# First RMS norm over partitions instead of rows: inputs loaded with features on partitions, sums by a product with ones

## The reference, cut to what matters

```python
def rms_norm(x, g):
    y = x * rsqrt(mean(x * x, axis=-1) + RMS_EPS)
    return y * g

u = rms_norm(x, g_pre) @ w_in + b_in          # q, k, v, pool input, two gates
# windowed attention over k, v (new tokens also see cache_k_win, cache_v_win)
# causal pooling over the pool input (new tokens also see state_pool)
m = sigmoid(ga) * (attn @ w_attn_up) + sigmoid(gp) * (pool @ w_pool_up)
h = x + rms_norm(m @ w_out, g_post_mix)
f = square(relu(rms_norm(h, g_pre_mlp) @ w_mlp_up)) @ w_mlp_down
y = h + rms_norm(f, g_post_mlp)
```

## Time and profile before

| what | value |
|---|---|
| median of 3 runs | 1433.7 us (1433.47 to 1434.33) |
| profiled execution, span from first to last instruction | 1431.3 us |
| around the span (median less span) | 2.4 us |
| PE busy | 1396.4 us, 98% |
| DVE, ACT, POOL busy | 38%, 32%, 11% |
| share of PE in the chain that ended last | 91% |

### The profile page before, as it was taken

How to read it: one execution, slowest core, us unless ns; L and a number is a source line. 1 busy time by engine, 2 the same in 40 slices (tenths; PEclk the granted TensorE clock), 3 DMA queues, 4 the chain that set the end, 5 groups by cost and what they waited for, 6 DMA issues and landing times.

```text
span 1431.3 us, 21460 instructions
## 1 busy us (share of the span) xinstructions
PE 1396.4 (98%) x8647; PEld 1366.2 (95%) x8647; DVE 543.1 (38%) x971; ACT 455.1 (32%) x891; POOL 161.8 (11%) x192
## 2 busy tenths in 40 slices
PE   6999999999999999999999999999999999999996
PEld 5999989999999999989999999999999999999986
DVE  5355541322222244687323323323223233232367
ACT  6354542311111143454224032141240321412423
POOL 3000565000000002441000000000000000000054
PEclk9999998999999999999999999999999999999997
DMA  9100000111111124130111111111011010111103
GB/s 303 39 30 16 31 16 30 49 45 44 45 45 45 45 60 118 45 96 15 32 43 50 42 42 52 36 44 59 29 59 44 29 59 29 44 58 34 56 1 125
DMA packets 28788, 74.56 MB, mean 52 GB/s; under 512 B 2722, under 2 KB 12088, under 8 KB 28703
## 3 DMA queue, kind: packets, MB, share of 16 engines
q1 hardware_dynamic: 19207, 65.84, 14.2%
q10 hardware_dynamic: 8400, 4.46, 1.2%
q0 software_dynamic: 1120, 3.39, 0.7%
HBM read 68.85 MB, written 5.92 MB: 52 GB/s over the span
## 4 chain that ended last, share of the span: by engine, by line
PE 91%; DVE 4%; DMA 2%; ACT 1%; issue 1%; POOL 0%; SPq 0%; ACTq 0%; DVEq 0%; POOLq 0%
PE ps L1238 28%; PE ps L1239 28%; PE ps L1240 28%; PE ps L1257 3%; PE ps L1388 2%; DVE acc L1201 1%; DVE hh L1206 1%; DMA xrow<-in_x_prompt 1%; DMA xre<-in_x_prompt 1%; PE ps L1451 0%; DMA xre_s<-in_x_sample 0%; DVE rsy L1090 0%; PE ps L1350 0%; DVE acc L1143 0%; PE ps L1397 0%
## 5 line engine op out<-in xcount | busy, mean ns | idle before, releaser
L1238 PE MATMUL ps<-xn,wr 128*128 128x384 f32 (+1 forms) x1344 | 443.8, 330 | 2.3 <-issue 1.5
L1239 PE MATMUL ps<-xn,wr 128*128 128x384 f32 (+1 forms) x1344 | 441.2, 328 | 0.0
L1240 PE MATMUL ps<-xn,wr 128*128 128x384 f32 (+1 forms) x1344 | 440.8, 328 | 0.0
L1238 PEld LDWEIGHTS ps<-xn,wr 128*128 128x128 f32 x1344 | 254.1, 189 | 3.7 <-issue 3.2
L1239 PEld LDWEIGHTS ps<-xn,wr 128*128 128x128 f32 x1344 | 254.1, 189 | 0.0
L1240 PEld LDWEIGHTS ps<-xn,wr 128*128 128x128 f32 x1344 | 253.8, 189 | 0.0
L1238 PE MATMUL ps<-ff,wr 128*128 128x384 f32 (+2 forms) x720 | 237.8, 330 | 0.0
L1239 PE MATMUL ps<-ff,wr 128*128 128x384 f32 (+2 forms) x720 | 236.8, 329 | 0.0
L1240 PE MATMUL ps<-ff,wr 128*128 128x384 f32 (+2 forms) x720 | 236.4, 328 | 0.0
L1126 DVE TENSOR_TENSOR ff<-sqa,ff 128x384 fp32r<-128x384 f32 (+1 forms) x96 | 51.5, 537 | 267.3 <-ACT ff L795 267.0
L1143 DVE TENSOR_TENSOR acc<-acc,ps 128x384 f32<-128x384 f32 (+2 forms) x168 | 88.6, 530 | 167.4 <-PE ps L1240 166.7
(11 more groups left out here) (215 smaller groups left out, 1619.6 us busy)
## 6 DMA issues: line engine op xcount, KB each, us to landing
raw<-in_weights SPq DMA_DIRECT2D x106, 512.0 KB, 3.5
xrow<-in_x_prompt SPq DMA_DIRECT2D x8, 512.0 KB, 9.9
xre<-in_x_prompt ACTq DMA_DIRECT2D x8, 512.0 KB, 5.7
out_y_prompt<-yrow SPq DMA_DIRECT2D x8, 512.0 KB, 2.6
bias_rev<-bias_by_distance POOLq DMA_DIRECT2D x1, 1024.0 KB, 10.4
gbc<-in_norm_pre_mix SPq DMA_DIRECT2D x1, 512.0 KB, 6.1
vcache<-in_cache_v_win POOLq DMA_DIRECT2D x1, 512.0 KB, 8.8
kcache<-in_cache_k_win SPq DMA_DIRECT2D x1, 512.0 KB, 11.1
```

Of the source, the lines that this page charges most:

```text
L1238: pe.matmul(out, wh, rh, start=(i == 0), stop=False)
L1239: pe.matmul(out, wh, rl, start=False, stop=False)
L1240: mm = pe.matmul(out, wl, rh, start=False, stop=(i == last))
```

## The change

x, the key cache and the pool state are laid out on the host with features on partitions, behind the weights (units `U_XT`, `U_XS`, `U_KC`), and the vectors as 128 columns. x is loaded as `xin [128, 8, 1088]`: for chunk 0 in four loads of two features each, for chunks 1 and 2 in one load each. The norm then sums over partitions and tiles: ACT squares feature by feature (`x_square`), DVE (chunk 0) or POOL (chunks 1 and 2) adds the eight squares to `xsum`, PE multiplies by ones (`x_total`), ACT takes the root of 128x384 (`x_root`), DVE inverts 128x384 (`x_invert`) and scales feature by feature in pairs into `xsc` (`x_scale`); ACT copies hi and DVE subtracts for lo. K groups wait per feature. All turns of x, vectors, key cache and state are gone. The residual adds x from `xre` in SBUF, loaded with features on partitions, one load a chunk (two for the last).

```diff
-            x_load(0)
-            sp.dma_start(gbc[:, :], I["norm_pre_mix"].to_broadcast([P, D])).then_inc(gbc_in, 16)
-            sp.dma_start(vecrow[:, :], I["vectors"]).then_inc(vec_in, 16)
-            x_load(1)
+            for i in range(2):
+                x_load(i, 2 * i, 2 * i + 2, 0)
+            sp.dma_start(vec[:, 0:V_EPS], I["vectors"]).then_inc(vec_in, 16)
+            unit(U_K, 0)
+            for i in range(2, 4):
+                x_load(i, 2 * i, 2 * i + 2, 0)
...
             unit(U_V, 1)
+            x_load(4, 0, KD, 1)
+            x_load(5, 0, KD, 2)
...
+            def add_x_squares(c):
+                for k in range(1, KD):
+                    pool.wait_ge(x_sq, KD * c + k + 1)
+                    pool.wait_ge(x_add, 7 * c + k - 1)
+                    w = CH[c][1]
+                    pool.tensor_tensor(xsum[:, 0:w], xsum[:, 0:w], xsq[k % 2][:, 0:w], ALU.add).then_inc(x_add, 1)
...
+            def x_square(c, k):
...
+                if k >= 3:
+                    act.wait_ge(x_add, 7 * c + k - 2)
+                act.activation((xsq[k % 2] if k else xsum)[:, 0:CH[c][1]], xin[:, k, cs(c)], ACT.Square).then_inc(x_sq, 1)
+
+            def x_root(c):
+                w = CH[c][1]
+                act.wait_ge(x_sum, c + 1)
...
+            for k in range(KD):
+                x_square(0, k)
             split(U_K)
...
+            x_root(0)
+            act.wait_ge(vec_in, 16)
+            for k in range(KD):
+                x_high(0, k)
+                if k == 1:
+                    split(U_V)
+                if k >= 3:
+                    x_square(1, k - 3)
+            for k in range(5, KD):
+                x_square(1, k)
             in_group(U_K, 0)
...
+            def x_scale(c, k0):
+                w = CH[c][1]
+                for k in (k0, k0 + 1):
+                    if KD * c + k >= 2:
+                        dve.wait_ge(x_lo, KD * c + k - 1)
+                    dve.scalar_tensor_tensor(out=xsc[k % 2][:, 0:w], in0=xin[:, k, cs(c)], scalar=vec[:, V_G0 + k:V_G0 + k + 1],
+                                             in1=xrs[c % 2][:, 0:w], op0=ALU.mult, op1=ALU.mult).then_inc(x_t, 1)
+                for k in (k0, k0 + 1):
+                    dve.wait_ge(x_hi, KD * c + k + 1)
+                    dve.tensor_tensor(xn[:, 1, k, cs(c)], xsc[k % 2][:, 0:w], xn[:, 0, k, cs(c)].bitcast(f32),
+                                      ALU.subtract).then_inc(x_lo, 1)
...
-                        dve.wait_ge(xr_t, KD * c + k + 1)
-                        dve.tensor_tensor(h, h, ps[:, 5 + k % 2, 0:w], ALU.add).then_inc(n_h, 1)
+                        if k == 0:
+                            dve.wait_ge(xr_in[c], 16 if c < NC_ - 1 else 32)
+                        dve.tensor_tensor(h, h, xre[:, k, cs(c)], ALU.add).then_inc(n_h, 1)
...
-                        x_again(st - 1, m)
```

More of the change, by code:

```diff
@@ L266, in build @@
         n_sum, n_sd, n_rs, n_t, n_h, n_sq, n_add = (sem("n_" + n) for n in ("sum", "sd", "rs", "t", "h", "sq", "add"))
-        n2_t, n2_hi, n2_lo, xr_in, xr_t = (sem(n) for n in ("n2_t", "n2_hi", "n2_lo", "xr_in", "xr_t"))
+        n2_t, n2_hi, n2_lo = (sem(n) for n in ("n2_t", "n2_hi", "n2_lo"))
+        xr_in = [sem(f"xr_in{c}") for c in range(NC_)]
         f_sq, f_hi, f_lo = sem("f_sq"), sem("f_hi"), sem("f_lo")
@@ L417, in _ @@
-            sp.dma_start(state_in[:, :], I["state_pool"][0].rearrange("b s n -> (b s) n")).then_inc(st_in, 16)
-            for r in range(5, RT):
-                x_load(r)
+            unit(U_V, 1)
+            x_load(4, 0, KD, 1)
+            x_load(5, 0, KD, 2)
+            sp.dma_start(xin[:, :, SEQ:ROWS], I["weights"][U_XS][:, 0:KD * SROWS].rearrange("p (k n) -> p k n", n=SROWS))\
+                .then_inc(x_in[5], 16)
+            sp.dma_start(kxT[:, :, 0:WIN], I["weights"][U_KC].rearrange("p (b n) -> p b n", n=WIN)).then_inc(kc_in, 16)
@@ L621, in _ @@
             act.wait_ge(eps_set, 1)
-            act.activation(rs[:, 0:1], eps, ACT.Sqrt).then_inc(x_sd, 1)
+            act.activation(xrs[0][:, 0:1], eps, ACT.Sqrt).then_inc(x_sd, 1)
             act.wait_ge(x_sd, 1)
-            x_stats(0)
-            x_stats(1)
-            x_high(0)
-            x_stats(2)
+            for k in range(KD):
+                x_square(0, k)
             split(U_K)
-            x_high(1)
-            x_stats(3)
-            x_high(2)
-            split(U_V)
-            x_stats(4)
-            x_stats(5)
-            act.wait_ge(kc_t, 1)
-            act.activation(kxT[:, :, 0:WIN], ps[:, 6:8, :].rearrange("p a (b n) -> p (a b) n", n=P), ACT.Copy)\
-                .then_inc(kc_r, 1)
-            x_high(3)
-            x_stats(6)
-            x_high(4)
-            act.wait_ge(vec_r, 1)
-            in_group(U_K, 0)
-            x_high(5)
-            x_stats(7)
-            in_group(U_V, 0)
-            x_high(6)
-            x_stats(8)
-            x_high(7)
-            in_group(U_K, 1)
-            x_high(8)
-            in_group(U_V, 1)
+            x_root(0)
[8 more added lines that the diff above has]
+                x_square(1, k)
+            in_group(U_K, 0)
+            x_root(1)
+            for k in range(KD):
+                x_high(1, k)
+                if k == 1:
+                    in_group(U_V, 0)
+                if k >= 2:
+                    x_square(2, k - 2)
+            for k in range(6, KD):
+                x_square(2, k)
+            in_group(U_K, 1)
+            x_root(2)
+            for k in range(KD):
+                x_high(2, k)
+                if k == 1:
+                    in_group(U_V, 1)
             in_group(U_K, 2)
@@ L940, in in_group @@
                                          op0=ALU.add, op1=ALU.subtract).then_inc(freed["D"], 1)
-            dve.wait_ge(gbc_in, 16)
-            x_scale(0)
-            x_scale(1)
-            x_low(0)
-            dve.wait_ge(vec_t, 1)
-            dve.tensor_copy(vec[:, 0:62], ps[:, 6, 0:62]).then_inc(vec_r, 1)
-            x_scale(2)
-            lo(U_K)
+            for k in range(1, KD):
+                dve.wait_ge(x_sq, k + 1)
+                dve.wait_ge(x_add, k - 1)
+                dve.tensor_tensor(xsum[:, :], xsum[:, :], xsq[k % 2][:, :], ALU.add).then_inc(x_add, 1)
+            lo(U_K)
+            dve.wait_ge(vec_in, 16)
+            x_invert(0)
+            x_scale(0, 0)
+            lo(U_V)
+            for k0 in (2, 4, 6):
+                x_scale(0, k0)
             dve.wait_ge(brow_p, 1)
@@ L1269, in _, with x_total, kv_group @@
-            pe.wait_ge(ident_set, 1)
-            x_turn(0)
-            pe.wait_ge(vec_in, 16)
-            turn(ps[:, 6, 0:62], vecrow[:, :], 62).then_inc(vec_t, 1)
-            x_turn(1)
+            def x_total(c):
+                pe.wait_ge(x_add, 7 * (c + 1))
+                pe.matmul(ps[:, 2 + c, 0:CH[c][1]], ones[:, :], xsum[:, 0:CH[c][1]], start=True, stop=True).then_inc(x_sum, 1)
+            def kv_group(n, c):
+                g = g_in(n, c)
+                need(n)
+                bank_free(g)
+                for k in range(KD):
+                    if n == U_K:
+                        pe.wait_ge(x_lo, KD * c + k + 1)
+                    wh, wl = wtile(n, k)
+                    rh, rl = rows(xn, k, c)
+                    out = ps[:, bank_of(g), 0:CH[c][1]]
+                    pe.matmul(out, wh, rh, start=(k == 0), stop=False)
+                    pe.matmul(out, wh, rl, start=False, stop=False)
+                    mm = pe.matmul(out, wl, rh, start=False, stop=(k == KD - 1))
+                mm.then_inc(done, 1)
@@ L1289, in _ @@
[L1289 to L1297 removed]
+            x_total(0)
+            kv_group(U_K, 0)
             kv_group(U_V, 0)
[L1299 to L1300 removed]
+            x_total(1)
             kv_group(U_K, 1)
[L1302 removed]
```

193 lines of the change are left out of this document (64 added, 129 removed).

## The result

| kernel | median, us | ratio to the kernel before (95%) |
|---|---|---|
| before, 4 runs | 1433.6 (1432.7 to 1434.3) | |
| changed, 4 runs | 1454.2 (1451.7 to 1457.7) | 1.0156 (1.0134 to 1.0178) |

The change makes the kernel 1.56% slower. The sign was forecast; the size was not: 1442.3 us was forecast, and 1454.2 lies 5.7 us above the range.

The account below looks back on a forecast made before the run. PE, busy 98% of the 1431.3 us span, was taken as the bound. 1431.3 + 16.9 (head) - 8.3 (residual stage) = 1439.9, with 2.4 around the span 1442.3 us; range 1436.5 to 1448.5.

Parts of the forecast that it names:

- The sign: Whole kernel: the change makes it slower, given 0.88.
- The five idle microseconds at the start of K1: Head: PE idle for about 5 us behind the second product with ones, at 36 to 42 us.
- the pace of the pairs: Head: K0 goes at the pace of feature pairs, 2.25 us a pair without collisions or squares, not of PE.
- The forecast's lower bound of the head: Head: if no collision and no square costs anything, the loss falls from 16.9 to 11.3 us.
- The head's size: Head: Q0 ends at 73.9 us instead of 56.99, 16.9 us later.
- Last features: 12.4: Head, load: chunk 0's last features of x land at 12.4 us, 0.4 of it for 1.5 KB runs.
- rival (b): PE at its slower level in V0 and V2/Q0: plus 3.5 to 7 us, 1446 to 1449; 13%.
- the adds' collisions: Head: scalings that meet POOL's adds take 1.36 us instead of 0.6.
- The residual stage: Residual stage: turns and waits removed from PE give a gain of 8.3 us, bounds 6 and 10.5.
- the old 4.65 us: Residual stage, chunk 1: a DVE step is 4.65 us, busy throughout, longer than a group of 320 columns (3.5).
- rival (a): Residual stage: full exclusion of DVE and POOL, chunk 1's step 6.5 us, gain 2.8, time 1447.8; 15%.
- its first sum is not late: Residual stage, chunk 0: the first sum isn't late, so the chunk gives its full 2.6 us.

Follow-up runs that it names:

- e13: Changed kernel with chunk 0's x loaded first, x's squares summed by PE, and chunk 0's sums issued ahead of the bias table's product: 1441.1 us, ratio 1.0062.
- e3: Changed kernel with chunk 0's x loaded ahead of the vectors and K's weight unit: 1449.9 us, ratio 1.0128.
- e10: Changed kernel with GpSimd's four small early loads issued behind its adds of chunk 1's squares: 1448.2 us, ratio 1.0115.
- e7: Changed kernel with unneeded products placed where PE waits in the head: 1451.9 us, ratio 1.0139.
- e4: Kernel before with only the new residual stage, POOL's adds of squares there done over one column: 1419.0 us (1 run).
- e11: Changed kernel with chunk 0's x loaded first and GpSimd's four small loads issued late: 1446.5 us, ratio 1.0104.
- e6: Changed kernel with POOL's adds of squares in head and residual stage done over one column (the narrow adds): 1432.7 us (1 run).
- e14: Changed kernel, chunk 0's x loaded first, squares of x and h summed by PE, chunk 0's sums ahead of the bias table's product: 1434.3 us, ratio 1.0018.

## Why the prediction was right or wrong

**The sign and the mechanism of the head: right, and shown.** The five idle microseconds at the start of K1 are there (5.15), so is the pace of the pairs. The forecast's lower bound of the head, without collisions, was 11.3 us, and e13, without adds, measures 11.9; that the two are so near is luck. The bound had K0 start at 20.3 and each sum behind V0; e13 starts K0 at 17.87 and takes the sums of the next chunk along with K and V, and still needs 51.0 us from there to vT's turn, where the bound had 48.0.

**The head's size: 16.9 forecast, 23.9 measured; 7.0 short.** Step by step along PE's rows:
- The product with ones: forecast at 14.0 (last add done 13.95), measured 16.96, so 3.0. The failed step is "Last features: 12.4"; ACT could square them only from 15.13. The rate was taken from the two queues of the page, as if 1.5 KB runs alone filled the queue. The vectors and the last loads of x shared the engines with GpSimd's loads. e3 and e10 show that x was late and that order alone cures it (3.9 and 4.0 us).
- The first feature of K0: 20.3 and 23.89, so 0.6 more, mostly the product with ones at the slower level (1.65 us).
- The product of chunk 1: begins at 35.9 in the forecast (36.5 is its end) and at 41.85, 2.35 more. Of these 0.65 are K0's, and 1.7 V0's, forecast at 4.2 us; it takes 5.9 (35.96 to 41.85), with its first products 0.32 us apart. This is rival (b), half true: the prediction bounded it at 3.5 us in V0 and left it out of the sum. e7 could not settle what it costs there, since it left V0 partly slow.
- The first feature of K1 0.3 more, the sum of chunk 2 0.2, the end 0.6.

The forecast gave 1.9 + 2.5 + 1.2 = 5.6 us to the adds' collisions, to squares between the hi copies and to POOL's last adds. The narrow adds show 7.1. e3 against e13, with the same loads, shows 8.2, but e13 also drops DVE's adds and starts the next sums earlier. So the term was right in kind and 1.5 us low.

**The residual stage: 8.3 forecast, 4.7 measured.** The three chunks: 1.2, -0.7 and 4.2 us, forecast 2.6, 0.5 and 5.2, so 1.4, 1.2 and 1.0 short. In chunk 1 the step that failed is the one taken at the old 4.65 us. It is 6.85, near the 6.5 of rival (a), and the sum waits 6.58 us instead of 5. The prediction had noted that the new add "reads two SBUF tiles and can lengthen POOL's adds" and charged 0.5 us for it. It also let chunk 0 keep its 2.6, because "its first sum is not late"; but its second sum was, and PE waited 1.24 us for POOL's. And it took the products behind the wait at full speed: from the second sum of chunk 1 to the next sum are 13.3 us, before 11.9. These 1.4 us are PE at its slower level behind a wait of 6.58 us, which is rival (b)'s mechanism at a place where the prediction didn't look for it. The rule of the Trainium skill ("SBUF — State Buffer", "Who interferes with whom") is that a DVE instruction with two SBUF inputs and a GpSimd one that reads SBUF exclude each other; the rival built on it had 15%. In this trace it holds: the add of x goes from 1.02 to 2.52 us a pair once it reads SBUF, and didn't move while it read PSUM. The row that I held against it, the lo part of 1.21 us that didn't grow, is none. Such a lo part is seen alone beside POOL's adds four microseconds later, at the end of chunk 1 before the change, where DVE has nothing behind it:

```profile
619.85 1.21 DVE L893 TENSOR_TENSOR wo<-raw,wo 128x1024 fp32r<-128x1024 f32 x1
```

```profile
620.10 2.95 POOL L552 TENSOR_TENSOR ssb<-ssb,sqb 128x384 f32<-128x384 f32 x2 [0.36 <-ACT sqb L775]
```

The lo part began first and kept its 1.21 us, and POOL's pair took 2.95 us instead of 2.0. It was POOL that stood still there. The stage gives 4.7 and not the 2.8 of that rival, since only one of the three steps meets POOL from end to end (the one before it is 634.34 - 630.38 = 4.0). e4 shows the cause: without full adds on POOL the new stage is 11.1 us shorter. The prediction also speaks of four short waits in the old stage; it names three, and the trace has three.

**The rest:** 1.3 us between the head and the first sum, 0.5 back behind it, and 2.9 instead of 2.4 us between span and median. 7.0 + 3.6 + 1.3 - 0.5 + 0.5 = 11.9 us, the miss. The 1.3 lies in the attention stage, which the change doesn't touch, in a stretch where PE goes at its slower level. The view by stretches, before (215 to 225) and changed (235 to 245 and 245 to 255):

```profile
215.00:225.00 10.00, 10.00 (x50) 7.04 (x50) 1.01 (x4) 0.45 (x2) 4.17 (x5) 0.51 0.16 52
```

```profile
235.00:245.00 10.00, 9.37 (x61) 4.98 (x61) 2.66 (x4) 1.86 (x3) 6.92 (x7) 0.63 0.19 54
245.00:255.00 10.00, 10.00 (x48) 9.62 (x48) 1.36 (x5) 1.36 (x5) 1.29 (x2) 0.69 0.01 2
```

With the slower level at half clock, the missing shares make (0.49 + 0.02) x 10 x 2 = 10.2 us of it before (0.98 from 225 to 235) and (0.37 + 0.31) x 10 x 2 = 13.6 after. Other kernels with the same attention show the same tie. The granted clock over the 25 us around that stretch is 0.80 before, in e3 and in e11, and from vT's turn to the first sum they take 505.1 us; it is 0.73 in the changed kernel and in e13, with 506.4; and 0.86 in e6 with 503.4. So the 1.3 us go with the clock, 3.4 us more at half the pace, which can cost up to 1.7; what sets the length of the stretch stays open. Of the spread of the changed kernel's times, 6 us, 3 lie in the span and the rest around it; e14's 6 us lie in the span, and no run says why, nor why e13's are only 1.7 us apart.

## What to carry to other kernels

A norm over partitions turns work that ran row block by row block into one chain per chunk, and whatever engine it feeds waits for that chain at every chunk's start; price it from the first feature, not from the sum of the work. Before taking work off the bounding engine, ask which engine was hidden behind it: here POOL's adds beside DVE cost the new stage 11 us, and the old one about 1. An operand moved from PSUM to SBUF can itself start such a collision. Sums of squares over features need neither: products with ones that accumulate in PSUM took the adds off POOL and gave 6.3 of those 11 us back (96.7 to 90.4). And a wait of 5 or 6 us on PE cost more than itself here: the products behind it ran at half the pace for some microseconds.
